# A table of token numbers loaded before the experts' weights, and two weight loads that no longer wait for the stored rows

## The reference, cut to what matters

```
h2 = rmsnorm(x, ffn_norm)                       # 512 x 1024
group  = top-1 of softmax(h2 @ w_rg + b_rg)     # 4 groups
expert = top-2 of 8 within the group            # 32 experts in all
combine[token, expert] = g1 * g2                # two weights for each token
for e in range(32):
    he = silu(h2 @ w_gate[e]) * (h2 @ w_up[e])  # 1024 -> 256
    y += combine[:, e] * (he @ w_down[e])       # 256 -> 1024
out = rmsnorm(x + y, final_norm)
```

## Time and profile before

| | us |
|---|---|
| median of 3 runs (lowest to highest) | 1333.78 (1329.61 to 1334.21) |
| time of the profiled execution | 1330.58 |
| its span | 1328.8 |
| PE busy in the span | 1267.5 (95%) |
| DVE, ACT, POOL busy | 663.1, 524.1, 538.6 |
| a `dn` load, issue to landing, median of 32 | 16.3 |

### The profile page before, as it was taken

The page is one execution under the profiler, slowest core; times in us unless marked ns, Lnnn a source line. Parts: engine busy times, 40 slices in busy tenths (PEclk is TensorE's granted clock), DMA queues, the critical chain, the costliest instruction groups (busy, mean ns, idle before and its releaser), DMA issues. The chain is left out here.

```text
span 1328.8 us, 20589 instructions
## 1 busy us (share of the span) xinstructions
PE 1267.5 (95%) x7788; PEld 921.3 (69%) x7788; DVE 663.1 (50%) x1358; ACT 524.1 (39%) x1121; POOL 538.6 (41%) x552
## 2 busy tenths in 40 slices
PE   7999999999999999989999999999989999999985
PEld 6766777878888877767888987777758833333332
DVE  5545995147751587973775441454454611111115
ACT  4312343356652343444665343575452221111111
POOL 0213698444445456875334431575361201111121
PEclk9999999999999999999999999999989999999998
DMA  9782111140003131112000222221036889999995
GB/s 393 300 305 96 48 34 48 62 158 2 1 27 133 64 118 64 48 64 95 2 2 33 97 96 72 96 88 64 32 138 235 330 330 410 416 411 401 395 387 215
DMA packets 47121, 209.58 MB, mean 158 GB/s; under 512 B 7767, under 2 KB 10199, under 8 KB 33696
## 3 DMA queue, kind: packets, MB, share of 16 engines
q1 hardware_dynamic: 38800, 194.59, 38.1%
q0 software_dynamic: 5760, 10.27, 2.1%
q10 hardware_dynamic: 2448, 3.21, 0.8%
HBM read 201.46 MB, written 17.30 MB: 165 GB/s over the span
## 5 line engine op out<-in xcount | busy, mean ns | idle before, releaser
L438 POOL TENSOR_TENSOR wlo<-raw,whi 128x512 fp32r<-128x512 f32 x102 | 141.2, 1389 | 141.6 <-ACT whi L426 131.6
L3431 PE MATMUL ps<-gu,XT 128*64 128x512 f32 x608 | 137.6, 600 | 5.7 <-DMA gu<-in_w_gu_dram 3.1
L426 ACT ACTIVATE whi<-raw 128x512 fp32r<-128x512 f32 x124 | 76.6, 628 | 144.0 <-PE ps L881 112.3
L1165 DVE SCALAR_TENSOR_TENSOR z<-glu,small,z 128x798 f32<-128x798 f32 (+1 forms) x120 | 132.6, 1153 | 0.8
L881 PE MATMUL ps<-hxh,whi 128*128 128x512 f32 x304 | 128.5, 423 | 1.7 <-ACT whi L426 1.3
L881 PE MATMUL ps<-hxh,wlo 128*128 128x512 f32 x304 | 119.9, 394 | 2.1 <-POOL wlo L438 2.1
L881 PE MATMUL ps<-hxl,whi 128*128 128x512 f32 x304 | 120.1, 395 | 0.0
L3431 PEld LDWEIGHTS ps<-gu,XT 128*64 128x64 f32 x608 | 45.0, 138 | 85.5 <-issue 78.8
L1708 POOL TENSOR_SCALAR P<-P,stat 128x768 f32<-128x768 f32 (+1 forms) x80 | 65.5, 821 | 72.3 <-DVE stat L1670 71.2
L1617 ACT ACTIVATE P<-ps,stat 128x768 f32<-128x768 f32 (+1 forms) x80 | 65.1, 814 | 59.2 <-DVE stat L1663 58.5
L1663 DVE TENSOR_REDUCE stat<-ps 128x1 f32<-128x768 f32 (+1 forms) x72 | 66.6, 926 | 22.6 <-PE ps L1568 22.2
(11 more groups left out here) (849 smaller groups left out, 3179.5 us busy)
## 6 DMA issues: line engine op xcount, KB each, us to landing
gu<-in_w_gu_dram SPq DMA_DIRECT2D x64, 1024.0 KB, 11.4
raw<-in_w_in_dram SPq DMA_DIRECT2D x66, 512.0 KB, 3.3
dn<-in_w_dn_dram SPq DMA_DIRECT2D x32, 1024.0 KB, 16.3
wgate<-in_w_mod_dram SPq DMA_DIRECT2D x16, 1024.0 KB, 7.6
raw<-in_w_out_dram SPq DMA_DIRECT2D x24, 512.0 KB, 3.3
wmod<-in_w_mod_dram SPq DMA_DIRECT2D x4, 2048.0 KB, 15.0
ybuf<-zero SPq DMA_DIRECT2D x1, 4096.0 KB, 12.6
yin<-ybuf SPq DMA_DIRECT2D x4, 1024.0 KB, 9.2
```

Source lines behind the costliest of these rows:

```text
L426: e.activation(K.hi[i][:, half(h)], K.raw[i % 2][:, half(h)], ACT.Copy).then_inc(*q.up("hi", i, h))
L438: e.tensor_tensor(K.lo[i][:, half(h)], K.raw[i % 2][:, half(h)], K.hi[i][:, half(h)].bitcast(F32), ALU.subtract).then_inc(*q.up("lo", i, h))
L1165: e.scalar_tensor_tensor(o, x, weight, o, ALU.mult, ALU.add).then_inc(*q.up("conv", l, i, j))
L3431: m = e.matmul(s[o, :], x[:, k, o], gu[:, k, :], start=k == 0, stop=k == KT - 1, skip_group_check=True)
```

## The change

The load of `iota` moves ahead of eight loads of weights on SP. In `more_loads` the wait for the last store of rows is gone, so that the next two loads (gu3 and gu4) wait only for what `experts_load` itself asks for. The three after them still wait for the first gather.

```
         e.dma_start(R.rc[:, :], d["rc"]).then_inc(*q.land("rc"))
+        e.dma_start(R.iota[:, :], d["iota"]).then_inc(*q.land("iota"))
         experts_load(S, 8)
-        e.dma_start(R.iota[:, :], d["iota"]).then_inc(*q.land("iota"))
 
     def more_loads():
 
-        for n, before in ((2, ("h2d", T2 - 1)), (3, ("first.gather", 0))):
-            for w in q(before):
-                e.wait_ge(*w)
-            experts_load(S, n)
+        experts_load(S, 2)
+        for w in q(("first.gather", 0)):
+            e.wait_ge(*w)
+        experts_load(S, 3)
     last_walk(S, loads=loads, more_loads=more_loads)
```

## The result

The changed kernel takes 1338.12 us (median of 13 runs, 1333.84 to 1341.44), the kernel before 1332.08 (13 runs, 1329.43 to 1334.21). The ratio is 1.0045, with a 95% interval of 1.0033 to 1.0058: slower by about 6 us, 4.4 to 7.7 by the interval. The prediction was 1331.8, range 1327.5 to 1336.0. It was wrong in time and in sign: it had the change 2 us faster.

The account below looks back on a forecast made before the run. The end was set by a full DMA stream whose restart waits for PE's first expert. iota 0, PE's earlier first rows -0.65 and the clock -1.4 gave -2.0 us: 1331.8 from the median 1333.78, range 1327.5 to 1336.0.

Parts of the forecast that it names:

- What bounds the experts: Experts' stage: a full DMA stream sets the end; its restart waits for PE's first pairs to free places.
- The rival of the whole lead: Experts' weight stream: gu3's full 8.5 us lead reaches the end, giving 1325.3; chance 0.05.
- `iota`: Table load on SP, moved ahead of eight weight loads: worth 0, its issue hidden by SP's 14.4 us stand.
- The last store: Block 3's store of rows: 8.6 us in weight traffic in place of 2.9, delaying L2977 on DVE by 1.6 us.
- a wait of over 2.3 us: At L2977 on DVE: a wait for the last store this long would show the forecast wrong.
- The other rival: Last store: even sharing makes it 4.2 us, L2977 is not delayed, 3.7 us gained, 1330.1; chance 0.17.
- The gather: First gather before the experts: 3.5 us with free DMA engines in place of 6.9, bounds 3.3 and 6.9.
- The clock: PE's first 32 expert multiplications: clock stays up, 1.4 us gained; bounds 0 and a loss of 1.4.
- Two of the signs: PE at the first expert: hardly a stand before turning the first rows, and first 32 multiplications in 7.1 us.
- The slower rival: Last two stores of rows land one after the other in weight traffic: up to 4.2 us lost, 1338.0; chance 0.13.
- D: Delay of L2977 on DVE from the last store's later landing: 1.6 us, bounds 0 and 6.5.
- the same: Whole kernel: time within about 0.5% (6.7 us) of the kernel before, given probability 0.92.

Follow-up runs that it names:

- the kernel with its own place: Changed kernel with block 3's rows in block 1's buffer, so L2977 waits only for block 0's store, against the kernel before: ratio 0.9996.
- The runs with the stand filled: 12 more warming calls on PE, in the changed kernel (1.0004) and in the kernel before with added DVE work (1.0008), against the kernel before.
- those with it open: The changed kernel (1.0045) and the kernel before with ones_at computed twice more on DVE (1.0047), without added warming calls, against the kernel before.
- the half dose: Changed kernel with only gu3 early and gu4 again behind the last store, against the kernel before: 1332.28 us, ratio 0.9998.
- The run with 21 calls: Changed kernel with block 3's rows in block 1's buffer and WARM 21 in place of 16, against the kernel before: 1333.05 us, ratio 1.0005.

## Why the prediction was wrong, point by point

**What bounds the experts: right as far as it goes.** Places are full and DMA idle until PE gets on, then DMA is full. gu3 went out 8.5 us earlier and nothing of it reached the end; what moved PE's first expert (+4.5 at the load of gu6) moved the end (+3.9). The rival of the whole lead is out. Whether from there on the full stream of weights or PE itself sets the end was not taken apart: both start later by the same amount, and PE waited for weights only 3.1 us before and 2.3 after.

**`iota`: right**, 0, shown by the run with it alone.

**The last store: right in kind, small in size.** I took 8.6 us, it was 9.6, and the wait on DVE was 2.7 in place of 1.6. Block 2's store (9.0) went ahead of it in the same traffic; whether that made the difference was not tested. The prediction had named a wait of over 2.3 us as a sign that it was wrong. The other rival, that queues share the DMA engines evenly and the store is not slowed, fell with it: even one load ahead made it 8.0. With it falls the use of the round-robin rule of the Trainium skill ("DMA: Bandwidth & Descriptors", section "Queues, rings and completion order") as a sum: the runs do not agree with the 4.2 us that the prediction drew from it, whatever the turns between the queues are.

**The gather: wrong, without effect.** I took 3.5 us with free engines; it took 4.8 here and 6.0 where nobody waited. PE was not ready for it in the changed kernel. With the stand of 1.46 us that it left, and the clock that fell behind it, it accounts for most (1.5 + 1.4) of the 3.7 us that the kernel with its own place did not gain.

**The clock: this is the step that failed.** The prediction put PE's clock down as a gain of 1.4 us, since the stand of 2.31 us before the first rows would go, and gave "a loss of 1.4, if PE's new stand of 1.6 us before L2977 makes it fall there too" as a bound only. The 1.4 was read off the first expert multiplications (8.46 against 7.09), where I took the clock to be low throughout. It was low only in their first part, 0.50 from 1066 to 1068 and back at 1.00 from 1069, so 1.4 us is the price of some 3 us at the low clock and no bound for a longer stretch:

```profile
1068.00:1069.00 1.00, 1.00 (x6) 0.42 (x4) 0.00 (x0) 0.00 (x0) 0.00 (x0) 0.74 1.02 426
```

In the changed kernel the stand became 2.7 us, the clock fell there, and it stayed at 1.2 GHz from 1058 to 1070 through work that is all on the path: the first list 3.47 - 1.98 = 1.5 us, the second 3.68 - 1.99 = 1.7, the warming row 6.04 - 3.84 = 2.2, together 5.4 against a bound of 1.4. The sum of the change for PE's first rows is then 2.7 + 5.4 = 8.1, less the 2.31 us that PE had stood for, 5.8 (5.9 read); less 1.4 for the first expert, 4.5 (4.5 read at gu6). The runs with the stand filled (1.0004 and 1.0008) against those with it open (1.0045 and 1.0047) show this term by itself. Two of the signs that the prediction gave came true, no stand before the first rows and 7.09 us for the first multiplications; they were the gains, and they came for the wrong reason, because PE was late itself.

**The slower rival** gave 1338.0, near the 1338.12 measured, but that is luck: it had D = 6.5 from two stores in a row and no clock; D was 2.7 and the clock made the rest. A ratio of 1.0045 is still within the 0.5% that the prediction called the same (0.92), though 13 runs of each kernel tell it from no change. The range did not reach it, because the loss by the clock had been bounded by what the clock could give back elsewhere and not by the length of the work behind the new stand.

## What to carry to other kernels

Where an early transfer shares the DMA engines with a small store that someone waits for, price the store by its time in such traffic, compare its landing with the moment it is needed, and count the margin: half a us late cost nothing that could be measured here, 2.5 to 2.7 us late cost 5 to 6. When a change makes a new stand on PE, ask what PE does right after it on the path, and price all of that at half clock; then take off what PE would have stood for later anyway (2.3 us here, and 1.4 for a fall of the clock that came later before). A price read off one short stretch at the low clock is no bound for a longer one. A buffer of its own for what the store reads, or multiplications that nobody reads and that last through the stand, each took the whole loss away.

## What the runs showed of the hardware

The last store, of 512 KB, took 2.9 us with the DMA engines nearly free and 9.3 to 9.6 among the loads of gu3 and gu4, and still 8.0 behind gu3 alone (2 MB).

A fall of PE's clock does not need a long stand: in the half dose it fell around 1056, after stands of 0.53 and 0.37 us among small multiplications, though the kernel before had stands of 0.63 and 0.37 there and kept it. And it came back while PE ran nothing but small multiplications, there (0.66 in the window from 1062 to 1063, 1.00 from 1063) and in the changed kernel (0.72 from 1070 to 1071, 1.00 from 1071).

The first gather, of 128 rows, took 4.6 to 4.8 us in six kernels, in five of them with hardly any weights moving, and 5.8 to 6.0 in the two with block 3 in its own place, with none moving. With weights in its first part it took 4.6 in the half dose and 5.8 to 6.9 in the kernel before and the one with `iota` alone. In the kernel with its own place an instruction fetch was under way at the same time. DMA queues there in a window of 0.15 us from 1058.6 (packets, MB, share of 16 engines):

```profile
q8 instruction: 1, 0.02, 80.2%
```

One packet of the instruction queue took 1.9 us (80.2% of 16 x 0.15); in the changed kernel one at 1067.7 took 0.95 (59.2% of 16 x 0.1 in a window of 0.1 us). The run with 21 calls had one of about 2 us (2.0% of 16 x 6 us), the run with the stand filled and the loads early had none and took 4.8. That such a packet is the cause of the extra 1.2 us was not tested.

After PE had stood for 1.6 us before the first rows, the clock was kept in one execution of the kernel before and it had fallen in the other, after 2.31 us. PE's timeline of the former:

```profile
1063.18 1.09 PE L3418 MATMUL ps<-ident,h 128*128 128x128 f32 x8 [1.58 <-DMA h<-h2d,kept]
1065.55 7.09 PE L3431 MATMUL ps<-gu,XT 128*64 128x512 f32 x32 [1.28 <-DVE XT L3543]
```

In the kernel with its own place it fell after 1.46 us, with `iota` alone after 1.31. So the length of such a stand decides nothing by itself, and a clock that falls in one profile is not sure to fall in the next.
